# A two-block transformer kernel on one core: another order of loads and norms at its start, and the inverse root of its second norm applied behind the first matmul of the MLP

## The reference

```
mod = silu(c) @ w_mod + b_mod            # six vectors of 1024: sh1, sc1, g1, sh2, sc2, g2; the same for c_ctx
h  = rms(x,  norm1) * (1 + sc1) + sh1    # 512 x 1024
hc = rms(xc, norm1) * (1 + csc1) + csh1  # 256 x 1024, the context
P, Pc = project(h), project(hc)          # w_in, 1024 columns in and 2064 out: Fourier part, q, k, v, delta part, gate z, gates
... attention, a gated delta rule in chunks (both directions), a Fourier mix
x = x + g1 * (cat @ w_out)
x = x + g2 * (max(h2 @ w_ff1, 0)**2 @ w_ff2)   where h2 = rms(x, norm2) * (1 + sc2) + sh2
```

## Time and profile before

| | |
|---|---|
| median of three runs | 3279.53 us (3270.61, 3279.53, 3281.13) |
| the profiled execution | 3272.58 us, of which the span is 3270.8 us |
| PE busy, share of the span | 96% |
| VectorE (DVE), ScalarE (ACT) busy | 54%, 34% |
| mean granted clock of TensorE | 0.984 of full speed |

### The profile page before, as it was taken

One profiled execution on the slowest core, in us unless ns is written; L12 is line 12 of the kernel. 1 busy time (PEld: TensorE's weight loads), 2 busy tenths in 40 slices (PEclk: granted clock), 3 DMA queues, 4 the chain that ended last, 5 costly groups with the idle time before them and its releaser, 6 DMA issues.

```text
span 3270.8 us, 42718 instructions
## 1 busy us (share of the span) xinstructions
PE 3148.9 (96%) x17856; PEld 2494.2 (76%) x17856; DVE 1772.1 (54%) x2414; ACT 1116.9 (34%) x1578; POOL 63.2 (2%) x65
## 2 busy tenths in 40 slices
PE   7788899899999999999999999999999999999997
PEld 4666864788888888776788888888887767888886
DVE  4535654544355434687764344753446877643446
ACT  3332235333243222425442223432233354422233
POOL 0002310000000000000000000000000000000000
PEclk8899999999999999999999999999999999999999
DMA  6231000232222322221223322223222212223222
GB/s 246 93 116 64 29 28 1 78 97 97 97 97 97 97 97 91 89 88 45 85 91 103 97 97 87 103 101 103 93 88 93 78 52 84 97 97 97 97 87 74
DMA packets 81935, 290.09 MB, mean 89 GB/s; under 512 B 9552, under 2 KB 11216, under 8 KB 81232
## 3 DMA queue, kind: packets, MB, share of 16 engines
q1 hardware_dynamic: 81744, 287.36, 26.2%
HBM read 285.23 MB, written 2.10 MB: 88 GB/s over the span
## 4 chain that ended last, share of the span: by engine, by line
PE 91%; DVE 5%; issue 2%; ACT 2%; DMA 1%; POOL 0%; SPq 0%; DVEq 0%; ACTq 0%; POOLq 0%
PE PS L1378 78%; PE PS L1460 3%; PE PS L1696 1%; PE PS L1659 1%; PE PS L1639 1%; PE PS L1698 1%; DVE XD L2145 1%; PE PS L1393 1%; PE PS L1717 1%; PE PS L1589 1%; PE PS L1706 1%; DVE SM L2321 0%; PE PS L1678 0%; ACT SPL L1747 0%; PE PS L1413 0%
## 5 line engine op out<-in xcount | busy, mean ns | idle before, releaser
L1378 PE MATMUL PS<-HS,SPL 128*128 128x512 f32 (+1 forms) x7752 | 1805.0, 393 | 8.2 <-DVE HS L2077 7.3
L1378 PEld LDWEIGHTS PS<-HS,SPL 128*128 128x128 f32 (+1 forms) x7752 | 1455.7, 189 | 330.0 <-issue 19.9
L2029 DVE TENSOR_TENSOR SPL<-RAW,SPL 128x1024 fp32r<-128x1024 f32 (+1 forms) x491 | 584.0, 1193 | 722.2 <-ACT SPL L1747 718.4
L1747 ACT ACTIVATE SPL<-RAW 128x1024 fp32r<-128x1024 f32 (+1 forms) x491 | 503.0, 1028 | 843.4 <-PE PS L1378 843.2
L1378 PE MATMUL PS<-FF,SPL 128*128 128x512 f32 x2880 | 654.6, 389 | 0.0
L1378 PEld LDWEIGHTS PS<-FF,SPL 128*128 128x128 f32 x2880 | 540.5, 188 | 112.3
L2410 DVE SCALAR_TENSOR_TENSOR CA<-AP__136,CW,CA 128x512 f32<-128x512 f32 x240 | 180.0, 750 | 6.2
L1930 ACT ACTIVATE FF<-TMP 128x512 fp32r<-128x512 f32 x88 | 55.7, 633 | 235.3 <-DVE TMP L2380 235.3
L1924 ACT ACTIVATE SA<-SA 128x512 f32<-128x512 f32 x88 | 55.5, 633 | 191.7 <-DVE SA L2370 191.7
L2370 DVE TENSOR_TENSOR SA<-PS,R 128x512 f32<-128x512 f32 x88 | 60.5, 691 | 98.8 <-PE PS L1378 98.5
L2321 DVE TENSOR_REDUCE SM<-PS 128x1 f32<-128x768 f32 (+2 forms) x96 | 61.7, 643 | 67.9 <-PE PS L1699 35.7
(11 more groups left out here) (289 smaller groups left out, 2220.4 us busy)
## 6 DMA issues: line engine op xcount, KB each, us to landing
RAW<-in_w_ff_in SPq DMA_DIRECT2D x176, 512.0 KB, 3.6
RAW<-in_w_in SPq DMA_DIRECT2D x88, 512.0 KB, 3.7
RAW<-in_w_ff_out SPq DMA_DIRECT2D x80, 512.0 KB, 3.5
RAW<-in_w_ff SPq DMA_DIRECT2D x64, 512.0 KB, 3.6
MW<-in_w_mod SPq DMA_DIRECT2D x48, 512.0 KB, 4.7
RAW<-in_w_out SPq DMA_DIRECT2D x24, 512.0 KB, 3.7
RAW<-in_w_ple_gate SPq DMA_DIRECT2D x16, 512.0 KB, 3.6
XT<-in_xT SPq DMA_DIRECT2D x2, 2048.0 KB, 7.7
```

What stands on the lines that cost most here:

```text
L1378: m = pe.matmul(o, w[x][:, k, rows], r.T[:, r.k0 + k, y, 0:r.cols], start=r.start and k == 0 and (x, y) == (0, 0), stop=r.stop and k == r. ...
L1747: a.activation(SPL[:, s, 0, 0:n], RAW[:, s, 0:n], AF.Copy).then_inc(w_hi, 1)
L2029: v.tensor_tensor(SPL[:, s, 1, 0:n], RAW[:, s, 0:n], SPL[:, s, 0, 0:n], ALU.subtract).then_inc(w_lo, 1)
```

## The change

Three things, with nothing else moved by hand.

1. Loads on SP: the 8 first pieces of `w_mod` follow x directly; the context, dense pieces 1 to 3 and the small constants are issued after the last of the first 8 modulation pieces has been used (in the list: after its refill). Only dense piece 0 is fetched and split early.
2. The sum of squares of x is emitted inside the first modulation groups (k = 0). The norm of the context becomes a generator `context`, put in `behind` ahead of the first projection: its squares, root and modulation stand between the matmuls of two projections. The second of these is `w_in[7]`, which stood at the end of the projections before.
3. The second norm: the gain is applied to the residual on ScalarE as each slice comes (`gain_x`, tile `XG` = x * gain). After the last, ScalarE takes the root straight from PSUM with the scale and eps in the same instruction; HS becomes XG + shift * root, that is the normed x times the root; the reciprocal is taken after the 8 slices, and `relu` multiplies by it.

```diff
-    m_r = mean_square(XT, m_x, R[:, :], 512)
-    m_rc = mean_square(XC, m_xc, RC[:, :], 256)
...
         if k < 4:
             mod(k)
             mod(4 + k)
-        else:
+        if k == 0:
+            m_r = mean_square(XT, m_x, R[:, :], 512)
+        if k == 4:
             tick()
...
-    hc_ready = modulate(HC, range(8), lambda j: XC[:, j, :], lambda j: SCG[:, j, 1:2], lambda j: MOD[:, j, 1:2],
-                        RC[:, :], 256, [m_rc])
     catch_up()
+    hc_ready = []
+
+    def context():
+        u = single()
+        for j in range(8):
...
+            emit("square_sum", r)
+            if j % 2:
+                yield 1
...
+        emit("root_of", r)
+        give(u)
+        for j in range(8):
+            hc_ready.extend(modulate(HC, (j,), lambda j: XC[:, j, :], lambda j: SCG[:, j, 1:2],
+                                     lambda j: MOD[:, j, 1:2], RC[:, :], 256, [m_rc]))
+            if j % 2:
+                yield 1
...
     rate[0] = 2
+    behind.append(context())
     dense(W["w_in"][0], 8, HS, hx_ready, evac_to(FT, 0, "f"))
+    dense(W["w_in"][7], 8, HS, None, evac_to(DZ, 0, "z"))
+    while behind:
+        tick()
...
-    for j, T, blk, key in ((1, AQ, 0, "q"), (2, AQ, 2, "q"), (7, DZ, 0, "z")):
+    for j, T, blk, key in ((1, AQ, 0, "q"), (2, AQ, 2, "q")):
...
-            while ahead < min(r.p.i + 4 if r else 4, len(pieces)):
+            while ahead < min(r.p.i + 4 if r else 1, len(pieces)):
...
-        sp.dma_start(XC[:, :, :], D["ctxT"]).then_inc(landed["xc"], 16)
         for p in mod_pieces[:8]:
             fetch_mod(p)
-        for p in pieces[:4]:
-            fetch(p)
...
+        fetch(pieces[0])
...
             if r.p.i == 7:
+                fetch(pieces[1])
+                sp.dma_start(XC[:, :, :], D["ctxT"]).then_inc(landed["xc"], 16)
+                for p in pieces[2:4]:
+                    fetch(p)
...
+        def gain_x(r):
+            a.wait_ge(*r.mark)
+            a.wait_ge(s_scg, r.gain)
+            a.activation(XG[:, r.j, :], XT[:, r.j, :], AF.Copy, scale=SCG[:, r.j, 0:1]).then_inc(s_xg, 1)
+
+        def second_norm(r):
+            a.wait_ge(*r.use.mark)
+            a.activation(R[:, :], PS[:, r.use.b, :], AF.Sqrt, scale=1.0 / 1024, bias=vec("eps")).then_inc(free[r.use.b], 1)
...
+            v.scalar_tensor_tensor(out=TMP[:, r.slot, :], in0=R[:, :], scalar=r.shift, in1=XG[:, r.j, :], op0=ALU.mult,
+                                   op1=ALU.add).then_inc(s_mu, 1)
...
+        def second_inverse(r):
+            v.reciprocal(R[:, :], R[:, :]).then_inc(s_inv, 1)
...
-            v.tensor_scalar(t, PS[:, r.use.b, :], 0.0, None, ALU.max).then_inc(free[r.use.b], 1)
+            v.wait_ge(*N.done)
+            v.scalar_tensor_tensor(out=t, in0=PS[:, r.use.b, :], scalar=0.0, in1=R[:, :], op0=ALU.max,
+                                   op1=ALU.mult).then_inc(free[r.use.b], 1)
```

More of the change, by code:

```diff
@@ L476, in build @@
                                  lambda j: MOD[:, j, 0:1], R[:, :], 512, [m_r])
-    hc_ready = modulate(HC, range(8), lambda j: XC[:, j, :], lambda j: SCG[:, j, 1:2], lambda j: MOD[:, j, 1:2],
-                        RC[:, :], 256, [m_rc])
     catch_up()
+    hc_ready = []
+    def context():
+        u = single()
+        for j in range(8):
+            r = Rec()
+            r.x, r.mark, r.use, r.j, r.n = XC[:, j, :], m_xc, u, j, 256
+            r.slot, r.after = tmp()
+            r.sq = count(s_sq)
+            slot_end[r.slot] = r.added = count(s_part) if j < 7 else u.mark
+            emit("square_sum", r)
+            if j % 2:
+                yield 1
+        r = Rec()
+        r.use, r.dst, r.n, r.width = u, RC[:, :], 256, 1024
+        r.root, m_rc = count(s_root), count(s_rms)
+        emit("root_of", r)
[5 more added lines that the diff above has]
+                yield 1
     ev_marks, qk_done = {}, {}
@@ L957, in ev_residual, with ev_first, ev @@
         return ev
-    for j in range(4):
-        hs_last = dense(W["w_out"][j], 8, HS, cat if j == 0 else None,
-                        ev_residual(j, lambda q: MOD[:, 16 + q, 0:1], None, None, None, True, None, [m_x2]))
-    m_r = stats_end(sts[0], R[:, :], ACC[:, :])
-    gain(32, "n2", 0, 8, [])
-    hx = modulate(HS, range(8), lambda j: XT[:, j, :], lambda j: SCG[:, j, 0:1], lambda j: MOD[:, 24 + j, 0:1], R[:, :],
-                  512, [m_r, hs_last])
+    gain(32, "n2", 0, 8, [])
+    gained = []
+    def ev_first(j):
+        plain = ev_residual(j, lambda q: MOD[:, 16 + q, 0:1], None, None, None, True, None, [m_x2])
+        def ev(i, u):
+            plain(i, u)
+            q = Rec()
+            q.j, q.mark, q.gain = 2 * j + i, u.rel, counted[s_scg]
+            gained.append(count(s_xg))
+            emit("gain_x", q)
+        return ev
+    for j in range(4):
+        hs_last = dense(W["w_out"][j], 8, HS, cat if j == 0 else None, ev_first(j))
+    N = Rec()
+    N.mark, N.use, N.done = sts[0], single(), count(s_inv)
+    emit("second_norm", N)
+    N.root = give(N.use)
+    hx = []
+    for j in range(8):
+        r = Rec()
+        r.j, r.waits, r.shift = j, [N.root, gained[j], hs_last], MOD[:, 24 + j, 0:1]
+        r.slot, r.after = tmp()
+        r.t, r.hi, r.lo = count(s_mu), count(s_muhi), count(s_mulo)
+        slot_end[r.slot] = r.lo
+        hx.append(r.lo)
+        emit("second_mod", r)
+        if j:
+            emit("second_lo", prev)
+        prev = r
+    emit("second_lo", prev)
+    emit("second_inverse", N)
     rate[0] = 0
@@ L1420, in rms @@
             pe.matmul(PS[:, r.use.b, 0:r.n], ones[:, :], r.acc, start=True, stop=True).then_inc(full[r.use.b], 1)
+        def second_norm(r):
+            pe.wait_ge(*r.mark)
+            opened(r.use)
+            pe.matmul(PS[:, r.use.b, :], ones[:, :], ACC[:, :], start=True, stop=True).then_inc(full[r.use.b], 1)
         def gate_turn(r):
@@ L2078, in modulate_lo, with second_mod, second_lo @@
                                    in1=r.T[:, r.j, 0, 0:r.n], op0=ALU.add, op1=ALU.subtract).then_inc(s_mulo, 1)
+        def second_mod(r):
+            for w in r.waits:
+                v.wait_ge(*w)
+            if r.after:
+                v.wait_ge(*r.after)
+            v.scalar_tensor_tensor(out=TMP[:, r.slot, :], in0=R[:, :], scalar=r.shift, in1=XG[:, r.j, :], op0=ALU.mult,
+                                   op1=ALU.add).then_inc(s_mu, 1)
+        def second_lo(r):
+            v.wait_ge(*r.hi)
+            v.tensor_tensor(HS[:, r.j, 1, :], TMP[:, r.slot, :], HS[:, r.j, 0, :], ALU.subtract).then_inc(s_mulo, 1)
+        def second_inverse(r):
+            v.reciprocal(R[:, :], R[:, :]).then_inc(s_inv, 1)
         def gates(r):
@@ L2708 @@
          "on": np.broadcast_to(x["o_norm_g"][0], (128, 64)), "fin": col(x["g_final_2"]),
-         "sel": (np.arange(128)[:, None] % 32 == np.arange(2)[None, :]).astype(f)}
+         "sel": (np.arange(128)[:, None] % 32 == np.arange(2)[None, :]).astype(f), "eps": np.full((128, 1), EPS, f)}
     for l in range(2):
```

25 lines of the change are left out of this document (17 added, 8 removed).

## The result

The changed kernel takes 3288.2 us (median of 7 runs, 3285.3 to 3288.6) against 3279.05 us before (7 runs, 3270.4 to 3282.6). The ratio is 1.0028, 95% interval 1.0019 to 1.0037: about 9 us, just under 0.3%, slower. I had forecast 3277.3 in a range of 3266 to 3287. The prediction was wrong in size and in sign, and the time lies beyond the range.

The account below looks back on a forecast made before the run. The prediction took the kernel to be bound by the amount of matmul work on PE (96% busy), which stays unchanged. Its terms, +4.0 - 2.0 - 4.2 = -2.2 us on the 3279.5 median, gave 3277.3, range 3266 to 3287.

Parts of the forecast that it names:

- Start, +4.0: From the loads through the first projection: later sums and squares cost +4.0 us net, from -1.6 to +6.
- the wait of 3.0 us: In the first projection, PE waits 3.0 us in front of the context's first sum, with 36 matmuls queued behind it.
- The gates' wait of 0.66 goes: After the first projection, PE's 0.66 us wait at the gates' product vanishes, as `w_in[7]` covers the context's normalisation.
- End of the projections, -4.0: At `w_in[7]`'s old place, the 2.13 us wait for the first query's norm and 1.9 of slow clock go: -4.0 us.
- A fourth norm among the inverses, +2.0: In the inverses, one more norm, 6.8 us on VectorE, partly holds up PE: +2.0 us, bounds nothing to 6.8.
- rival of reciprocals that stop the inverses: In the inverses, four reciprocals each hold PE 3.7 us and drop its clock: +15.7 in all, 3295 us; chance 0.05.
- Attention stage, no term at all: In the attention stage, behind the edited stretches, the forecast counted no change in time.
- Second norm, -4.2: At the second norm, the first slice no longer waits for scale, reciprocal and gain: -4.2 us, range -3 to -4.5.
- Sum: Whole kernel: the terms for start, end of projections with inverses, and second norm together give -2.2 us.

## Why the prediction was wrong, step by step

- *Start, +4.0.* Too large: the second piece ends 2.8 us later than in the trace that I read, 3.9 forecast, and the whole effect is +2.1 by medians, good to 5. The windows' +2.95 is for the change as a whole up to that mark, and 1.9 of it is modulation work that would have come later. The norm of x was ready 0.8 us earlier than I said (reciprocal's end 30.14, forecast 30.9), and the wait of 3.0 us came in two parts, 2.16 and 0.90. "The gates' wait of 0.66 goes" was wrong; it stayed to the hundredth, so the context's slices did not set it (three other traces name VectorE's split as its end). And I had priced the start from one form of it: in seven of thirteen traces the old one reaches the first projection 3 us later.
- *End of the projections, -4.0.* Half right: the wait of 2.13 is gone and the window is 4.93 us shorter, but 1.9 and 2.2 us of that are work that only moved. In its place PE now waits 1.85 us for a load of `w_mod` at 255.43 and 1.64 for `st` at 258.15, behind the first query's reciprocal (254.22 to 257.56); its idle time there went from 4.55 us to 3.94. I had moved the norm's chain and not asked what it would hold up where it landed.
- *A fourth norm among the inverses, +2.0, with all its 6.8 us as the upper bound.* This step failed, in size and in place. With the end of the projections it was to make -2.0, from -4.0 to +2.8; moving `w_in[7]` alone measured +7.7, good to 3. I had priced the norm as VectorE work that PE, among the inverses, either waits for or not. It isn't the reciprocal's length: without the long reciprocals the move still costs far over 2 us. What the traces show for certain is behind the inverses, where I had nothing: the scans take 6.03 us more, of which 2.2 are the last norm's own matmuls at full clock and 3.4 more idle time of PE (5.3 to 8.7 us), with the wait for its VectorE step and the one while a late DFT matrix loads. The 3.05 us more of the inverses may be luck. My rival of reciprocals that stop the inverses had the side (slower) right, with 0.05, and the mechanism wrong.
- *Attention stage, no term at all.* This failed too: banks that a shared counter hands out cost 4.0 us in the changed kernel, and 8.6 when given to the kernel before. A term of nothing for everything outside the edited stretches was never argued; the comparison of the two programs' steps doesn't show bank numbers, and I didn't ask for them.
- *Second norm, -4.2.* Right: -4.2 by medians, -4.39 by the traces. The Trainium skill (ScalarE: Activation LUTs, "What ACT_TABLE_LOAD costs") counts some 2.66 us with the drain; here the root started 1.41 us after its table load began, and would have started no earlier without the load, so the trace bears out the rows that I took and not that rule.
- *Sum.* By medians +2.1 + 7.7 + 4.0 - 4.2 = +9.6, measured +9.1. That is no test: the start's +2.1 is what the other medians leave, so the four add up by construction. Measured for themselves are +7.7, -4.2, and the banks. The base was right, since I added my sum to the median and not to the fast execution of the trace.

What stays open: why the scans and the stretch ahead of them take longer when the norms come later, and which step of the interleaved norms makes each of the waits of 2.08, 3.03 and 2.84 us. For the first two waits the runs exclude the reciprocals' length (2.08 and 3.04 with short ones; the third goes from 2.84 to 1.93), for all three the banks. What ends the wait of 2.50 us at 429.93 isn't shown by a releaser either; that the DFT load runs at that moment is all the trace says.

## What to carry to other kernels

A resource that a planner hands out in turn (banks, slots, queues) ties every step to every other: moving one projection in the start changed the banks, and the time, of steps 400 us later. Compare the assignments of the two programs everywhere, and give steps beside fixed users a bank of their own. A long piece of matmul work late in its stage is cover for whatever chain runs beside it; ask what falls out at the far end, with its matmuls and loads, before moving it. A term that is left over when the others are subtracted is not a measurement; a run of its own is. A wait's price need not be its length: 2.2 us of waits at the delta turns were worth 4.6 us (3 to 9).

## What was not expected of the hardware

The same wait of 1.75 us, before the same matmuls in the same banks, was followed by 3.4 us at TensorE's half level in one execution and by 17 us in another, 486 to 503 us, though PE was busy for nearly all of it from 488 on (3.00 of 3.00 us in the later windows). That alone makes 6 us between two executions. The old start has two forms 3 us apart in the same way: behind one wait of 1.60 us the clock fell in seven of thirteen traces (mean 0.64 in 29 to 31 us in that of `w_in[7]` early, 1.00 in the kernel before) and stayed full in six. Both fit the spread of the kernel before (3270 to 3283) and a profiled execution 7 us under the median, which had the quick form of both. A single profile of each kernel can't settle a difference of 0.2%.
